# Prompt attention with undivided probabilities: the division moved from the probability rows to the weighed sums

## The chip, the cores and the metric

One core of a Trainium2 chip. The time is what the device takes for one execution of the program, in microseconds (us). A core has TensorE (matrix products, PE in the profile, its weight loads PEld), VectorE (DVE), ScalarE (ACT), GpSimd (POOL) and SyncE (SP, which issues all DMAs here). SBUF is the on-chip memory of 128 partitions; PSUM has 8 banks of 512 f32 for each partition and takes TensorE's results.

## The reference, cut to what matters

One layer of a decoder with two token mixers, for a prompt of 1024 tokens and 8 samples of 8 tokens each. The change touches the prompt's attention only:

```python
def block(args):
    i, qlb, qrb = args
    s = (jnp.einsum('bqhr,bkr->bhqk', qlb, c_kv)
         + jnp.einsum('bqhp,bkp->bhqk', qrb, k_r)).astype(jnp.float32)
    qpos = i * Q_BLOCK + jnp.arange(Q_BLOCK)
    s = jnp.where(kpos[None, :] <= qpos[:, None], s, -jnp.inf)
    p = jax.nn.softmax(s, axis=-1).astype(c_kv.dtype)
    return jnp.einsum('bhqk,bkr->bqhr', p, c_kv)
...
a = jnp.einsum('bshr,rhv->bshv', o_lat, w_uv).reshape(B, S, MLA_WIDTH)
```

There are 8 heads; everything is f32. A softmax divides exp(s - max) by its sum over the keys, one sum for each query and head.

## The kernel before, in words

The program works through stages: input norms and projections, prompt attention, the samples' attention, the output projection, the feed-forward part (gate and up, then down) and the last norm. A product of f32 matrices is made of three products of split operands (`mm3`, lines 873 to 875: high by high, low by high, high by low); the high part is a copy (`hi` on ScalarE, line 1425), the low part a subtraction on VectorE or POOL.

Prompt attention is cut into 16 units (`UNITS`). Unit u belongs to the pair of heads u // 4, to head u // 2 % 2 of that pair, and to the block of 512 queries u % 2 (block 0 or 1). A block has four query tiles of 128 (qi 0 to 3), and block 0 sees four key tiles (kt), block 1 eight. Because of the causal mask, query tile qt needs only its first qt + 1 key tiles, so row 3 of a unit is 512 columns wide in block 0 and 1024 in block 1.

For each query tile: `score` on TensorE makes the scores in one of two pairs of PSUM banks, VectorE takes their maximum (L2113) and scales it (L2116), ScalarE makes the exponential into the SBUF tile `prob` and sums it in its accumulator (L1578, an ACTIVATE and an ACTIVATION_READ_ACCUMULATOR), and VectorE inverts the sum (L2102). Then the row of probabilities is multiplied by the inverse: rows 0 to 2 on POOL (`normalise`, L782), row 3 on VectorE (L2107). For each key tile, `turn` transposes the probabilities on TensorE (L1096) into PSUM bank 4 or 5, ScalarE copies the high part to `pTH` and VectorE subtracts to get `pTL` (L2129); `product` multiplies them by the values `hvH`, `hvL`, two key tiles later in TensorE's order, and adds up in PSUM bank 6 or 7 (by the unit's parity). The result, 64 rows by 512 queries, goes to `aT` by a ScalarE copy (`move_weighed`) during key tile 1 of the next unit.

The order on each engine is written out by hand. While unit u is weighed, the scores, maxima and exponentials of unit u + 1 are made, one query tile for each key tile (`row_at`): at key tiles 0 to 3, and in the last unit of a pair (u % 4 == 3) at key tiles 4 to 7, as its first four key tiles carry the query and key projections of the next pair (`query_key`, `move_gen`, `query_hi`, and `query_lo` on POOL). After such a unit come the values of the next pair (`values`). Before the last unit, TensorE makes the samples' queries (L1131). Every engine runs its own list in order; semaphores join them. TensorE's `turn(0)` of a unit waits for the multiplied rows (`s_pn`, `s_pd`), a `turn` or `product` for the subtraction of the tile (`t_free`), `product(0)` for the accumulator's release (`o_free`). DMAs are all issued by SyncE; attention itself needs few.

Of the kernel before, what the change touches and what calls it, by code (L numbers as in the profile page):

```python
# [22 lines left out]
ALU = mybir.AluOpType  # L23
# [107 lines left out]
def build(nc, d):  # L131
    ctx = ExitStack()
    with ctx:
# [28 lines left out]
        mx, nmx, sm, rsm = (small.put(n, [P, 4]) for n in ("mx", "nmx", "sm", "rsm"))  # L162
# [93 lines left out]
        ukT = Region(R0).put("ukT", [NOPE, H, KVR])  # L256

# [53 lines left out]
        def sem(name):  # L311
# [34 lines left out]
        s_ready, s_mx, s_nm, s_exp, s_rc, s_pn, s_pd = (  # L346
            sem("s_" + n) for n in ("ready", "mx", "nm", "exp", "rc", "pn", "pd"))
# [313 lines left out]
        def _(pool):  # L661
# [114 lines left out]
            def normalise(u):  # L776
                for qi in range(3):
                    r, qt = 4 * u + qi, 4 * (u % 2) + qi
                    n = P * (qt + 1)
                    row = prob[:, prob_at(qt):prob_at(qt) + n]  # L780
                    pool.wait_ge(s_rc, r + 1)
                    pool.tensor_tensor(row, row, rsm[:, r % 4:r % 4 + 1].broadcast_to((P, n)),  # L782
                                       ALU.mult).then_inc(s_pn, 1)

# [10 lines left out]
            normalise(0)  # L795
            for u in range(UNITS):
                p = u // 4
                if u % 4 == 3 and u < UNITS - 1:
                    query_lo(p + 1)
                if u < UNITS - 1:  # L800
                    normalise(u + 1)
                if u == 0:
                    pool.wait_ge(out_ckv, 16)
                    pool.wait_ge(n2_lo, 2 * NC)
                    for z in qz:
                        pool.memset(z[:, :, :, :], 0.0).then_inc(made_z, 1)
                if u % 4 == 3 and p + 2 < PAIRS:
                    head_pieces(p + 2)
# [61 lines left out]
        def _(pe):  # L870
# [209 lines left out]
            def weigh(u):  # L1080
# [5 lines left out]
                def turn(kt):  # L1086
                    x = tr_count(u) + kt
                    if x >= 2:
                        pe.wait_ge(t_free, x - 1)
                    for qi in range(max(0, kt - 4 * blk), 4):  # L1090
                        if kt == 0 and qi < 3:
                            pe.wait_ge(s_pn, 3 * u + qi + 1)
                        elif kt == 0:
                            pe.wait_ge(s_pd, u + 1)
                        at = prob_at(4 * blk + qi) + P * kt
                        last = nc.tensor.transpose(ps[:, 4 + x % 2, P * qi:P * qi + P], prob[:, at:at + P],  # L1096
                                                   ident[:, :])
                    last.then_inc(t_ready, 1)

                def product(kt):  # L1100
                    x = tr_count(u) + kt
                    c0 = P * max(0, kt - 4 * blk)
                    pe.wait_ge(t_free, x + 1)
                    if kt == 0 and u >= 2:
                        pe.wait_ge(o_free, u - 1)
                    mm3(ps[:, 6 + u % 2, c0:512], hvH[:, kt, :], hvL[:, kt, :], pTH[:, x % 4, c0:512],
                        pTL[:, x % 4, c0:512], kt == 0, kt == nk - 1).then_inc(pv_x, 1)

                for kt in range(nk + 2):
# [9 lines left out]
                    if kt >= 2:  # L1119
                        product(kt - 2)  # L1120
                    if qi is not None and row_late(u, kt):
                        score(u + 1, qi)
# [300 lines left out]
        def _(act):  # L1423
# [159 lines left out]
            def move_weighed(u):  # L1583
                p, hh, blk = u // 4, u // 2 % 2, u % 2
                act.wait_ge(pv_x, tr_count(u + 1))
                part = slice(VH * hh, VH * hh + VH)
                hi(aT[part, p, 512 * blk:512 * blk + 512], ps[part, 6 + u % 2, :]).then_inc(o_free, 1)

            def move_turned(u):
                blk = u % 2  # L1590
                for kt in range(4 * (blk + 1)):
# [12 lines left out]
                    if kt == 1 and u:  # L1604
                        move_weighed(u - 1)
# [27 lines left out]
            move_weighed(UNITS - 1)  # L1633
# [253 lines left out]
        def _(dve):  # L1887
# [206 lines left out]
            def invert(r):  # L2094
                s = slice(r % 4, r % 4 + 1)
                dve.wait_ge(s_exp, r + 1)
                u, qi = r // 4, r % 4
                if u and qi < 3:
                    dve.wait_ge(s_pn, 3 * (u - 1) + qi + 1)
                elif u:  # L2100
                    dve.wait_ge(s_pd, u)
                nc.vector.reciprocal(rsm[:, s], sm[:, s]).then_inc(s_rc, 1)  # L2102
                if qi == 3:
                    qt = 4 * (u % 2) + 3
                    row = prob[:, prob_at(qt):prob_at(qt + 1)]
                    dve.wait_ge(s_rc, r + 1)
                    nc.vector.tensor_scalar(row, row, rsm[:, s], None, ALU.mult).then_inc(s_pd, 1)  # L2107
# [10 lines left out]
            def move_turned(u):  # L2118
                blk = u % 2
                for kt in range(4 * (blk + 1)):  # L2120
# [5 lines left out]
                    if qi:  # L2126
# [3 lines left out]
                                            pTH[:, x % 4, c0:512], ALU.subtract).then_inc(t_free, 1)  # L2130
                    for i in gens_at(u, kt):
                        move_gen(u // 4 + 1, i)
# [13 lines left out]
            for u in range(UNITS):  # L2146
                p = u // 4
                move_turned(u)
                if u % 4 == 3 and u < UNITS - 1:
                    move_values(p + 1)  # L2150

# [35 lines left out]
            dve.wait_ge(s_pn, 3 * UNITS)  # L2187
            dve.wait_ge(s_pd, UNITS)
# [466 lines left out]
```

## Time and profile before

| | us |
|---|---|
| median of three runs | 1470.52 (1469.29, 1470.52, 1474.88) |
| the profiled execution | 1473.64 |
| its span | 1471.7 |
| prompt attention in it, about | 292 to 526 |

The span runs from the first to the last recorded instruction. Busy shares are of this span; matmul and weight load overlap, so their shares are not added. The granted clock (PEclk) is 1.00 at 2.4 GHz and 0.50 at 1.2 GHz. "Idle before" is the time an engine waited just ahead of an instruction, with the engine and line that ended the wait. The stage around the change is 16% of the span; behind it lie 947 us of samples' attention, projections and feed-forward that the change does not touch.

### The profile page before, as it was taken

What the parts mean: (1) busy time and instruction counts of PE and PEld (TensorE: products, weight loads), DVE (VectorE), ACT (ScalarE), POOL (GpSimd) and SP (SyncE); (2) the same over time, 40 slices, a digit from 0 to 9 for tenths busy, and PEclk for the clock granted to TensorE, in tenths of its full rate; (3) what the DMA queues carried; (4) which work ended last, traced back from release to release, by engine and by line L of the source; (5) the groups of instructions that cost most, each with busy time, mean ns of one, the idle gap of its engine ahead of it and who ended that gap; (6) DMA issues with size and microseconds to landing.
All of it is one profiled execution on the core that took longest, in us unless ns stands there. A gap on an engine that the chain in (4) does not pass through costs nothing.

```text
span 1471.7 us, 23463 instructions
## 1 busy us (share of the span) xinstructions
PE 1354.1 (92%) x9216; PEld 1259.0 (86%) x9216; DVE 827.0 (56%) x1304; ACT 506.6 (34%) x870; POOL 439.4 (30%) x278
## 2 busy tenths in 40 slices
PE   6979998799999898999669999999999989999987
PEld 4758898688888765899659999999999989999987
DVE  4793114666666432514765454434445547989975
ACT  3412212455655431301332222222222224444452
POOL 1161222434333202154644444444444410000000
PEclk9989999899999899999779999999999999999998
DMA  7011010200003532442012222222222249766503
GB/s 230 3 46 59 25 34 4 70 1 19 1 15 117 188 115 112 163 141 94 4 37 74 74 88 80 73 80 76 69 73 73 88 159 368 266 194 229 196 1 122
DMA packets 64376, 142.10 MB, mean 97 GB/s; under 512 B 7490, under 2 KB 14530, under 8 KB 63586
## 3 DMA queue, kind: packets, MB, share of 16 engines
q1 hardware_dynamic: 64290, 140.93, 28.1%
q8 instruction: 57, 0.93, 0.3%
q14 instruction: 29, 0.24, 0.1%
HBM read 118.35 MB, written 22.55 MB: 96 GB/s over the span
## 4 chain that ended last, share of the span: by engine, by line
PE 71%; DVE 15%; issue 4%; DMA 4%; POOL 2%; ACT 2%; SPq 0%; DVEq 0%; POOLq 0%; ACTq 0%
PE ps L873 21%; PE ps L874 21%; PE ps L875 21%; DMA araw<-in_w_dn 2%; PE ps L1096 2%; PE ps L881 2%; DVE x L1890 2%; PE ps L1159 1%; DVE aHL L2442 1%; DMA x<-in_x 1%; DVE bHL L2445 1%; PE ps L1202 1%; DVE mx L2113 1%; DVE bsum L2434 1%; DVE mL L2227 1%
## 5 line engine op out<-in xcount | busy, mean ns | idle before, releaser
L827 POOL TENSOR_TENSOR ws<-wraw,ws 128x1024 fp32r<-128x1024 f32 x55 | 136.5, 2483 | 199.9 <-ACT ws L1425 199.9
L873 PE MATMUL ps<-bHL,aHL 128*128 128x272 f32 x616 | 180.2, 293 | 11.5 <-DVE bHL L2445 11.5
L875 PE MATMUL ps<-bHL,aHL 128*128 128x272 f32 x616 | 179.0, 291 | 0.0
L874 PE MATMUL ps<-bHL,aHL 128*128 128x272 f32 x616 | 178.8, 290 | 0.0
L873 PEld LDWEIGHTS ps<-bHL,aHL 128*128 128x128 f32 x616 | 117.8, 191 | 13.0 <-DVE bHL L2445 13.0
L2308 DVE TENSOR_TENSOR bufP<-bufP,ps 128x544 f32<-128x544 f32 x66 | 47.5, 721 | 139.3 <-PE ps L875 137.1
L1425 ACT ACTIVATE ws<-wraw 128x1024 fp32r<-128x1024 f32 x55 | 58.3, 1061 | 181.9 <-PE ps L875 181.9
L874 PEld LDWEIGHTS ps<-bHL,aHL 128*128 128x128 f32 x616 | 117.8, 191 | 0.0
L875 PEld LDWEIGHTS ps<-bHL,aHL 128*128 128x128 f32 x616 | 117.6, 191 | 0.0
L827 POOL TENSOR_TENSOR ws<-wsum,ws 128x1024 fp32r<-128x1024 f32 x22 | 64.8, 2946 | 66.2 <-ACT ws L1425 66.2
L865 POOL TENSOR_TENSOR rt<-ms,mhalf 128x3 f32<-128x3 f32 (+1 forms) x3 | 3.1, 1039 | 265.3 <-DVE ms L2474 265.3
L2129 DVE TENSOR_TENSOR pTL<-ps,pTH 128x512 fp32r<-128x512 f32 (+1 forms) x96 | 53.1, 554 | 46.3 <-ACT pTH L1425 44.8
L782 POOL TENSOR_TENSOR prob<-prob,rsm 128x128 f32<-128x128 f32 (+5 forms) x48 | 49.7, 1042 | 96.7 <-DVE rsm L2102 96.7
L2308 DVE TENSOR_TENSOR bufC<-bufP,ps 128x544 f32<-128x544 f32 x42 | 30.3, 720 | 80.3 <-PE ps L875 72.9
L1425 ACT ACTIVATE aHL<-araw 128x512 fp32r<-128x512 f32 x66 | 41.7, 631 | 89.1 <-DVE araw L2417 59.9
L1425 ACT ACTIVATE pTH<-ps 128x512 fp32r<-128x512 f32 (+1 forms) x96 | 46.9, 490 | 52.1 <-PE ps L1096 51.1
L1096 PE MATMUL ps<-ident,prob 128*128 128x128 f32 x288 | 54.2, 295 | 11.5 <-DVE prob L2107 7.4
L873 PE MATMUL ps<-x4H,ws 128*128 128x272 f32 x176 | 52.3, 297 | 7.4 <-POOL x4L L832 7.4
L873 PE MATMUL ps<-x3H,ws 128*128 128x272 f32 x176 | 51.8, 294 | 6.9 <-DVE x3L L2278 6.9
L1578 ACT ACTIVATE prob<-ps,nmx 128x128 f32<-128x128 f32 (+3 forms) x64 | 47.4, 741 | 28.9 <-DVE nmx L2116 28.9
L873 PE MATMUL ps<-x1H,ws 128*128 128x272 f32 x176 | 52.2, 297 | 5.2 <-POOL x1L L832 5.2
L2113 DVE TENSOR_REDUCE mx<-ps 128x1 f32<-128x128 f32 (+3 forms) x64 | 48.1, 751 | 12.5 <-PE ps L1077 12.2
(356 smaller groups left out, 4509.9 us busy)
## 6 DMA issues: line engine op xcount, KB each, us to landing
araw<-in_w_dn SPq DMA_DIRECT2D x121, 256.0 KB, 3.3
wraw<-in_w_gu SPq DMA_DIRECT2D x44, 512.0 KB, 3.6
cp<-in_cache SPq DMA_DIRECT2D x64, 272.0 KB, 4.7
ab<-acts SPq DMA_DIRECT2D x34, 272.0 KB, 4.9
acts<-bufC SPq DMA_DIRECT2D x22, 272.0 KB, 2.1
x<-in_x SPq DMA_DIRECT2D x4, 1088.0 KB, 8.1
x2s<-x SPq DMA_DIRECT2D x8, 544.0 KB, 9.2
x<-x2s SPq DMA_DIRECT2D x8, 544.0 KB, 6.2
```

The costliest lines, as they stand in the source:

```text
L782: pool.tensor_tensor(row, row, rsm[:, r % 4:r % 4 + 1].broadcast_to((P, n)), ALU.mult).then_inc(s_pn, 1)
L827: pool.tensor_tensor(w[:, 1, :], w_source(j), w[:, 0, :], ALU.subtract).then_inc(cw_lo, 1)
L873: nc.tensor.matmul(out, wh, xh, start=start, stop=False)
L874: nc.tensor.matmul(out, wh, xl, start=False, stop=False)
L875: return nc.tensor.matmul(out, wl, xh, start=False, stop=stop)
L881: last = nc.tensor.matmul(ps[:, bank, 0:n], ones[:, :], sq[:, kk, 0:n], start=kk == 0, stop=kk == k - 1)
L1096: last = nc.tensor.transpose(ps[:, 4 + x % 2, P * qi:P * qi + P], prob[:, at:at + P], ident[:, :])
L1425: return nc.scalar.activation(out, x, ACT.Copy, scale=scale)
L1578: nc.scalar.activation(prob[:, prob_at(qt):prob_at(qt) + n], psf[:, 1024 * (r % 2):1024 * (r % 2) + n], ACT.Exp, bias=nmx[:, s:s + 1], sca ...
L2113: nc.vector.tensor_reduce(mx[:, s], psf[:, at:at + P * (qt + 1)], AX.X, ALU.max).then_inc(s_mx, 1)
L2129: nc.vector.tensor_tensor(pTL[:, x % 4, c0:512], ps[:, 4 + x % 2, c0:512], pTH[:, x % 4, c0:512], ALU.subtract).then_inc(t_free, 1)
L2308: nc.vector.tensor_tensor(halves(out[:, g, :]), halves(x[:, g, :]), pair(b + 2 * g), ALU.add).then_inc(added, 1)
```

## The change

Probabilities stay undivided. POOL's `normalise` and VectorE's multiplication of row 3 go. `turn(0)` waits for the exponentials. The inverse sums get eight columns, so that two units can hold theirs. At key tile 3 of a unit, behind `turn(3)` and `product(1)`, TensorE makes four transpositions (`row_factors`): the stationary operand is one column of inverse sums repeated 128 times, the moving one the identity, so that each of the 128 output rows holds the inverse sums of the 128 queries. They go to the PSUM bank that held the accumulator of the unit before. ScalarE copies 64 of these rows to `rinv` (`move_factors`, key tile 3), and no longer moves the weighed sums. VectorE does this now, multiplying them by `rinv` as it reads them (`move_weighed`, behind its subtraction at key tile 1 of the next unit).

```diff
-        mx, nmx, sm, rsm = (small.put(n, [P, 4]) for n in ("mx", "nmx", "sm", "rsm"))
+        mx, nmx, sm = (small.put(n, [P, 4]) for n in ("mx", "nmx", "sm"))
+        rsm = small.put("rsm", [P, 8])
...
+        rinv = Region(R0 + 1024).put("rinv", [P, 512])
...
-            def normalise(u):
-                for qi in range(3):
-                    r, qt = 4 * u + qi, 4 * (u % 2) + qi
-                    n = P * (qt + 1)
-                    row = prob[:, prob_at(qt):prob_at(qt) + n]
-                    pool.wait_ge(s_rc, r + 1)
-                    pool.tensor_tensor(row, row, rsm[:, r % 4:r % 4 + 1].broadcast_to((P, n)),
-                                       ALU.mult).then_inc(s_pn, 1)
...
-                        if kt == 0 and qi < 3:
-                            pe.wait_ge(s_pn, 3 * u + qi + 1)
-                        elif kt == 0:
-                            pe.wait_ge(s_pd, u + 1)
+                        if kt == 0:
+                            pe.wait_ge(s_exp, 4 * u + qi + 1)
...
-                    if kt == 0 and u >= 2:
-                        pe.wait_ge(o_free, u - 1)
+                    if kt == 0 and u:
+                        pe.wait_ge(s_rk, u)
...
+                def row_factors():
+
+                    pe.wait_ge(s_rc, 4 * u + 4)
+                    if u:
+                        pe.wait_ge(o_free, u)
+                    for qi in range(4):
+                        i = 4 * (u % 2) + qi
+                        last = nc.tensor.transpose(ps[:, 7 - u % 2, P * qi:P * qi + P],
+                                                   rsm[:, i:i + 1].broadcast_to((P, P)), ident[:, :])
+                    last.then_inc(s_rt, 1)
...
                     if kt >= 2:
                         product(kt - 2)
+                    if kt == 3:
+                        row_factors()
...
-            def move_weighed(u):
-                p, hh, blk = u // 4, u // 2 % 2, u % 2
-                act.wait_ge(pv_x, tr_count(u + 1))
-                part = slice(VH * hh, VH * hh + VH)
-                hi(aT[part, p, 512 * blk:512 * blk + 512], ps[part, 6 + u % 2, :]).then_inc(o_free, 1)
+            def move_factors(u):
+                act.wait_ge(s_rt, u + 1)
+                hi(rinv[VH:P, :], ps[VH:P, 7 - u % 2, :]).then_inc(s_rk, 1)
...
-                    if kt == 1 and u:
-                        move_weighed(u - 1)
+                    if kt == 3:
+                        move_factors(u)
...
             def invert(r):
-                s = slice(r % 4, r % 4 + 1)
                 dve.wait_ge(s_exp, r + 1)
-                u, qi = r // 4, r % 4
-                if u and qi < 3:
-                    dve.wait_ge(s_pn, 3 * (u - 1) + qi + 1)
-                elif u:
-                    dve.wait_ge(s_pd, u)
-                nc.vector.reciprocal(rsm[:, s], sm[:, s]).then_inc(s_rc, 1)
-                if qi == 3:
-                    qt = 4 * (u % 2) + 3
-                    row = prob[:, prob_at(qt):prob_at(qt + 1)]
-                    dve.wait_ge(s_rc, r + 1)
-                    nc.vector.tensor_scalar(row, row, rsm[:, s], None, ALU.mult).then_inc(s_pd, 1)
+                if r >= 8:
+                    dve.wait_ge(s_rt, r // 4 - 1)
+                nc.vector.reciprocal(rsm[:, r % 8:r % 8 + 1], sm[:, r % 4:r % 4 + 1]).then_inc(s_rc, 1)
+
+            def move_weighed(u):
+                p, hh, blk = u // 4, u // 2 % 2, u % 2
+                dve.wait_ge(pv_x, tr_count(u + 1))
+                dve.wait_ge(s_rk, u + 1)
+                part = slice(VH * hh, VH * hh + VH)
+                nc.vector.tensor_tensor(aT[part, p, 512 * blk:512 * blk + 512], ps[part, 6 + u % 2, :], rinv[VH:P, :],
+                                        ALU.mult).then_inc(o_free, 1)
...
+                    if kt == 1 and u:
+                        move_weighed(u - 1)
```

## Rows read from the trace of the kernel before

**Rows 1.** The page, part 1: busy time, share of the span, instructions.
```profile
PE 1354.1 (92%) x9216; PEld 1259.0 (86%) x9216; DVE 827.0 (56%) x1304; ACT 506.6 (34%) x870; POOL 439.4 (30%) x278
```
**Rows 2.** Stretches, all engines: length, busy us (instructions), PEclk, DMA share, GB/s.
```profile
292.00:526.00 234.00, 216.30 (x1305) 188.99 (x1306) 145.43 (x329) 131.75 (x301) 75.66 (x74) 0.94 0.16 54
```
**Rows 3.** Waits of TensorE in 292:526: us in total, times, longest.
```profile
PE ps L1096 <- DVE prob L2107: 7.4, 5, 2.0
```
**Rows 4.** Timeline of TensorE, gaps: start, length, instruction [idle before].
```profile
303.66 0.33 PE L1096 MATMUL ps<-ident,prob 128*128 128x128 f32 x1 [2.00 <-DVE prob L2107]
...
363.52 0.47 PE L1096 MATMUL ps<-ident,prob 128*128 128x128 f32 x1 [1.74 <-DVE prob L2107]
...
503.96 4.92 PE L1131 MATMUL ps<-qs,ukT 64*128 64x64 f32 x32 [2.10 <-ACT prob L1578]
```
**Rows 5.** Timeline, VectorE and ScalarE ahead of the gap's end in unit 5.
```profile
359.84 1.22 DVE L2113 TENSOR_REDUCE mx<-ps 128x1 f32<-128x1024 f32 x1
...
361.27 1.11 ACT L1578 ACTIVATE prob<-ps,nmx 128x1024 f32<-128x1024 f32 x1 [1.68 <-DVE nmx L2116]
...
362.29 0.19 ACT L1578 ACTIVATION_READ_ACCUMULATOR prob<-ps,nmx 128x1 f32 x1
...
362.71 0.75 DVE L2107 TENSOR_SCALAR prob<-prob,rsm 128x1024 f32<-128x1024 f32 x1
```
**Rows 6.** Timeline, the same steps before units 1, 0 and 15.
```profile
302.17 0.19 ACT L1578 ACTIVATION_READ_ACCUMULATOR prob<-ps,nmx 128x1 f32 x1
302.60 1.01 DVE L2107 TENSOR_SCALAR prob<-prob,rsm 128x1024 f32<-128x1024 f32 x1
...
292.29 0.19 ACT L1578 ACTIVATION_READ_ACCUMULATOR prob<-ps,nmx 128x1 f32 x1
293.25 0.33 PE L1096 MATMUL ps<-ident,prob 128*128 128x128 f32 x1 [0.22 <-DVE prob L2107]
...
503.62 0.19 ACT L1578 ACTIVATION_READ_ACCUMULATOR prob<-ps,nmx 128x1 f32 x1
```
**Rows 7.** VectorE's groups by shape in 292:526: busy us, mean ns, idle before.
```profile
L2081 DVE TENSOR_TENSOR kL<-ps,kH 64x512 fp32r<-64x512 f32 x12 | 8.2, 685 | 0.2
```
**Rows 8.** Timeline of VectorE in unit 4, key tiles 1 and 2.
```profile
356.14 0.54 DVE L2129 TENSOR_TENSOR pTL<-ps,pTH 128x384 fp32r<-128x384 f32 x1
356.84 1.09 DVE L2113 TENSOR_REDUCE mx<-ps 128x1 f32<-128x896 f32 x1 [0.15 <-PE ps L1077]
```
**Rows 9.** Timeline of TensorE: four transpositions and the product behind them.
```profile
310.29 0.60 PE L1096 MATMUL ps<-ident,prob 128*128 128x128 f32 x4
310.65 0.48 PE L873 MATMUL ps<-pTH,hvH 128*128 128x512 f32 x1
```
**Rows 10.** Line 1096 alone: ns min/median/max, first and last start.
```profile
L1096 PE MATMUL ps<-ident,prob x288: 270/273/475, 292.2 to 523.9; 128*128 128x128 f32 x144
```
**Rows 11.** ScalarE's groups by shape in 292:526.
```profile
L1425 ACT ACTIVATE aT<-ps 64x512 f32<-64x512 f32 x16 | 9.4, 586 | 1.1 <-PE ps L875 1.0
```
**Rows 12.** Timeline, unit 3: ScalarE at key tile 4, TensorE's wait behind.
```profile
340.12 0.58 ACT L1425 ACTIVATE pTH<-ps 128x512 fp32r<-128x512 f32 x1
...
342.45 0.41 PE L873 MATMUL ps<-kH,qH 128*128 128x384 f32 x1 [0.59 <-ACT prob L1578]
```
**Rows 13.** Timeline, unit 5: ScalarE's copy of tile 4, TensorE's product 4.
```profile
370.12 0.59 ACT L1425 ACTIVATE pTH<-ps 128x512 fp32r<-128x512 f32 x1
...
371.79 0.48 PE L873 MATMUL ps<-pTH,hvH 128*128 128x512 f32 x1
```
**Rows 14.** Stretches behind two gaps, as in rows 2: the clock.
```profile
362.50:366.50 4.00, 2.98 (x14) 2.98 (x15) 2.75 (x9) 1.79 (x5) 0.40 (x1) 0.57 0.02 4
57.00:61.50 4.50, 2.95 (x17) 2.24 (x16) 2.44 (x6) 0.40 (x1) 0.85 (x1) 1.00 0.00 0
```
**Rows 15.** Timeline of TensorE: two other gaps.
```profile
287.85 0.66 PE L873 MATMUL ps<-kH,qH 128*128 128x384 f32 x1 [1.64 <-ACT prob L1578]
...
59.55 0.71 PE L889 MATMUL ps<-diag,ones 128*128 128x128 f32 x4 [1.55 <-DVE diag L1919]
```

More of the change, by code:

```diff
@@ L343, in build @@
         vg_ready, vg_hi, vg_free = sem("vg_ready"), sem("vg_hi"), sem("vg_free")
-        s_ready, s_mx, s_nm, s_exp, s_rc, s_pn, s_pd = (
-            sem("s_" + n) for n in ("ready", "mx", "nm", "exp", "rc", "pn", "pd"))
+        s_ready, s_mx, s_nm, s_exp, s_rc, s_rt, s_rk = (
+            sem("s_" + n) for n in ("ready", "mx", "nm", "exp", "rc", "rt", "rk"))
         t_ready, t_hi, t_free, pv_x, o_free = (sem(n) for n in ("t_ready", "t_hi", "t_free", "pv_x", "o_free"))
@@ L794, in _ @@
             head_pieces(1)
-            normalise(0)
             for u in range(UNITS):
@@ L799, in _ @@
                     query_lo(p + 1)
-                if u < UNITS - 1:
-                    normalise(u + 1)
                 if u == 0:
@@ L1632, in _ @@
                     move_values(p + 1)
-            move_weighed(UNITS - 1)
             def sample_exp(g):
@@ L2150, in _ @@
                     move_values(p + 1)
+            move_weighed(UNITS - 1)
             def sample_max(g):
@@ L2185, in move_latents @@
                         "p (b h t) -> p b h t", b=2, h=H)).then_inc(o4, 1)
-            dve.wait_ge(s_pn, 3 * UNITS)
-            dve.wait_ge(s_pd, UNITS)
+            dve.wait_ge(s_rt, UNITS)
             def scale_heads(c, bank):
```

## The prediction

> **What bounds the kernel now.** I read the page first: TensorE is busy 92% of the span [rows 1]. Then the stretches: prompt attention fills 292 to 526 us, TensorE busy 216.3 of 234 us at a mean granted clock of 0.94, VectorE 145 us, ScalarE 132 us [rows 2]. So TensorE bounds this stretch, with gaps, and every instruction added to it is paid unless it falls in a gap. The waits say what ends the gaps: the largest single one is 7.4 us on the VectorE multiplication of row 3 (L2107) [rows 3]. The timeline puts them in place. Units go in fours of about 60 us. Unit 1 of a four (units 1, 5, 9, 13) opens with a gap: TensorE restarts at 303.66 and 363.52 after gaps of 2.00 and 1.74 us, each with a shorter wait on POOL just before it. Unit 15 opens with a 2.10 us gap that an exponential ends, not a multiplication [rows 4]. Only these four gaps can shrink; units 3, 7 and 11 open with score and query products of the next pair as cover, and the units of block 0 follow long products.
>
> **The four gaps.** In unit 5 the chain is: maximum over 1024 (359.84, 1.22 us), exponential (361.27, 1.11 us), its accumulator read (ends 362.48), reciprocal, multiplication (362.71, 0.75 us), transposition at 363.52 [rows 5]. After the change the transposition waits for the accumulator read alone. Before unit 15 that step takes from 503.81 to 503.96, 0.15 us [rows 4, 6], so here it could start at 362.63: 0.9 us earlier. In unit 1 the read ends at 302.36, the transposition started at 303.66 and could start at 302.5: 1.15 us earlier (the multiplication took 1.01 us there). In unit 0 the read ends 292.48 and the fourth transposition came at 293.25: 0.6 us earlier [rows 6]. POOL's 48 multiplications end no gap that would outlast this.
>
> But the maximum itself comes later in units 4, 8 and 12. VectorE now moves the weighed sums of the unit before, right behind its subtraction of key tile 1, and ahead of the maximum over 896. The nearest row for that move is a TENSOR_TENSOR of 64x512 from PSUM with an SBUF operand, 0.685 us [rows 7]. Between the subtraction's end (356.68) and the maximum (356.84, after 0.15 us of waiting on TensorE) VectorE has 0.3 us at most, counting overlaps [rows 8]; so some 0.4 us runs down the chain through the two maxima and two exponentials behind it. Gain there 0.9 - 0.4 = 0.5 us, three times. Unit 0 has no move, unit 1 keeps its 1.15. Together: -0.6 - 1.15 - 1.5 = -3.25 us. What is late next in all of them is the exponential.
>
> **Added on TensorE.** 64 transpositions, four a unit. Four of the same shape at the full clock take from 310.29 to the product at 310.65: 0.36 us [rows 9]; I take 0.4. Their stationary operand is one column repeated, which no row shows; the bounds are nothing (all in gaps) and 0.475 us each, the longest of the 288 [rows 10], 30 us in all; I take the near row because shape and moving operand are the same. In units 0, 4, 8, 12 and 14 they stand before a gap that VectorE and ScalarE end, so they are hidden. In 3, 7 and 11 they are hidden too, but by a wait that the next part makes longer. Paid in eight units: +3.2 us. If the cover of the five goes, +2.0 more. Their own waits cost nothing: the reciprocals are done before the unit opens, and the accumulator is freed two key tiles earlier. Behind them in TensorE's queue stand turn 4 and product 2.
>
> **Moved on ScalarE.** A copy of 64x512 leaves key tile 1 and another enters at key tile 3, both 0.586 us [rows 11]: no change in busy time, but in place. In units 3, 7 and 11 ScalarE is the late one exactly there: it starts the copy of turned tile 4 at 340.12, back to back with the query work, and TensorE then waits 0.59 us for exponential 0 of the next unit, until 342.45 [rows 12]. The new copy goes in between: 3 x 0.6 = +1.8 us. In units 1, 5, 9 and 13 it stands between exponential 3 and the copy of tile 4. That copy started at 370.12 [rows 13]; now maximum 3 is 0.3 to 0.5 us later (the move on VectorE) and the copy goes behind both, near 371.0; its subtraction (0.69) ends near 372.3, while turn 6, which needs it, would be ready some 0.4 us sooner (TensorE reaches product 4 at 371.79 now, 0.26 us behind turn 6, and 0.4 later with the added four). At the opening of these units the copy of the unit before also stands ahead of the first turned tile, some 0.3 us. I take 0.7 us, four times: +2.7 us rounded; bounds 0 (the VectorE multiplication of row 3 is gone at the same place and may pay for all of it) and 1.2 us each.
>
> **Unit 14.** The VectorE move delays the chain of maxima by some 0.6 us and the gap before unit 15 gets nothing back, since it waits for the exponential already: +0.6 us. POOL: its queue only gets shorter, and its query work stands in the same order. DMA queues are not touched.
>
> **The clock.** Behind each of the four gaps the granted clock is at 1.2 GHz for a while: 0.57 in the mean over 362.5 to 366.5, so some 3.4 of these 4 us [rows 14]. A gap of 1.64 us at 287.85 was followed by such a fall, one of 1.55 us at 59.55 was not, the clock staying 1.00 [rows 14, 15]. The gap before unit 1 shrinks to about 0.9 us, those before 5, 9 and 13 to about 1.4. Work of 3.4 us at half clock costs TensorE 1.7 us, but here ScalarE and VectorE stand close behind, and I let half of that come back to them: 0.9 us for each fall that stays out. I take unit 1 and one more: -1.8 us.
>
> Sum: -3.25 + 3.2 + 1.8 + 2.7 + 0.6 - 1.8 = +3.2 us. The profiled execution took 1473.64 us (span 1471.7 and 1.9 around it), so 1476.8; it is 3.1 us above the median of the three runs, 1470.52, and measured against that the forecast is 1473.7 us.
>
> A rule on the multiplication that goes: the Trainium skill, "SBUF — State Buffer", section "Who interferes with whom", says that VectorE and GpSimd share one port pair as an exclusive lock, taken by fp32 tensor_scalar in its two-port mode. The trace agrees as far as it goes: the same 1024 columns took 0.75 us in unit 5 and 1.01 in unit 1 [rows 5, 6]. By that rule the POOL work that goes frees nothing else, for the VectorE instructions that stay read PSUM; without it one could hope for a VectorE that is faster throughout.
>
> **Rivals.**
> 1. The clock falls behind all four gaps as before. For it: the gap of 1.4 us is close to the 1.64 that was followed by a fall, and new short gaps stand behind it. Against: unit 1, with 0.9. Sum +5.0: 1475.5 us. Chance 0.25.
> 2. Faster side: no fall is left and ScalarE and VectorE keep their places at no cost: -3.25 + 3.2 - 4 x 1.7 = -6.9: 1463.6 us. For it: a multiplication that goes took VectorE 0.75 us at 1024 columns, as much as a move brings. Against: it goes from the gap, and the move comes where VectorE is full. Chance 0.08, of which 0.03 beyond 0.5%.
> 3. Slower side: VectorE becomes the bound in block 0. There it worked without a break over two key tiles [rows 8]. If each of the 15 moves with work behind it is paid at 0.685, that is 10.3 us; with the transpositions (3.2), ScalarE (1.8) and the gains of units 0 and 1 (-1.75): +13.6, 1484.1 us. It decides from six full moves more than I count. Against it: even there VectorE waited 0.15 us for TensorE, and the multiplication that goes stood at the head of the same queue. Chance 0.12.
> 4. The transpositions of a repeated column are dear: 0.475 us each in 11 units, 20.9 us in place of 3.2: 1491 us. Nothing in the profile speaks for it. Chance 0.03.
> That the stalls don't move at all, since something other than the multiplication ends them, is excluded by the 0.06 us between its end and the transposition [rows 5].
>
> **The numbers.** The forecast has 0.52; its own range is 1471 to 1477. The range that takes in rivals 1, most of 2 and the near part of 3 is 1467 to 1482. About 0.5% (7.4 us) is what a measurement of this kernel can tell from no change. Faster by more: 0.03. Slower by more: 0.09 from rival 3 and 0.03 from rival 4. The rest, 0.85, is within it.
>
> **What would show it.** Right: the longest gap before units 5, 9 and 13 at 1.3 to 1.5 us, ended by the exponential; before unit 1 about 0.9; the four added transpositions some 0.4 us from the first to what follows; the wait near 342.45 grown to about 0.8; a new wait of 0.3 to 0.5 us at turn 6 of units 1, 5, 9, 13, ended by the subtraction. Wrong: VectorE moves of over 1 us, added transpositions that take longer than the others, a mean clock over attention above 0.97 (rival 2), or VectorE named at waits all over block 0 (rival 3).

## The result, and the profile after

The changed kernel takes 1477.00 us in the median of 20 runs, the kernel before 1472.74 in the median of 20: a ratio of 1.0027, 95% interval 1.0017 to 1.0037. By the ratio that is 4.0 us more, where 3.2 more were forecast; the interval leaves out 1, and the difference is below the half per cent that the prediction named as what a measurement can tell from no change.

The page after, parts 1 (busy time, share of the span, instructions) and 2 (the granted clock in 40 slices):

```profile
PE 1357.4 (92%) x9280; PEld 1263.1 (86%) x9280; DVE 822.8 (56%) x1304; ACT 508.6 (35%) x870; POOL 389.8 (26%) x230
...
PEclk8999999899999899999779999999999999999988
```

Against [rows 1]: POOL has 48 instructions and 50 us less, TensorE 64 instructions more. VectorE and ScalarE have kept their number of instructions and nearly their busy time. What changed is the place of the work.

The stretches of attention, and the four that lie behind the openings of units 1, 5, 9 and 13 (columns as in [rows 2]):

```profile
292.00:526.00 234.00, 214.49 (x1347) 188.02 (x1345) 138.59 (x325) 131.59 (x298) 25.54 (x26) 0.96 0.16 54
304.50:308.50 4.00, 4.00 (x27) 3.22 (x25) 2.69 (x9) 3.16 (x8) 0.00 (x0) 1.00 0.00 0
362.00:366.00 4.00, 3.52 (x23) 3.20 (x23) 3.66 (x10) 2.63 (x9) 0.00 (x0) 1.00 0.00 0
422.00:426.00 4.00, 3.53 (x25) 3.06 (x24) 3.20 (x11) 2.62 (x9) 0.00 (x0) 1.00 0.00 0
482.00:486.00 4.00, 3.52 (x23) 3.06 (x23) 3.20 (x9) 2.95 (x8) 0.00 (x0) 1.00 0.62 235
```

None of the four falls to 1.2 GHz is left in this execution, where [rows 14] had 0.57 over 4 us. The kernel is slower all the same. The waits of TensorE in 292:500 say where (us in total, times, longest):

```profile
PE ps L863 <- ACT prob L1579: 7.0, 12, 1.3
PE ps L1084 <- ACT prob L1579: 4.5, 4, 1.2
PE ps L1084 <- DVE pTL L2126: 2.8, 4, 0.9
```

The same stretch before had the 7.4 us of [rows 3] and two more that compare:

```profile
PE ps L873 <- ACT prob L1578: 3.1, 9, 0.6
PE ps L1096 <- POOL prob L782: 0.9, 4, 0.2
```

The waits on the multiplications are gone (8.3 us); 4.5 us on the exponentials stand at the same four places. But the scores (L863) wait 3.9 us more for an exponential to leave their bank, and a new wait of 2.8 us for VectorE's subtractions has come. The two in detail, timeline of all engines after (start, length, instruction [idle before]): first unit 3 at key tiles 3 and 4, then unit 1 at key tile 6:

```profile
337.32 0.60 ACT L1426 ACTIVATE rinv<-ps 64x512 f32<-64x512 f32 x1
337.94 0.60 ACT L1426 ACTIVATE pTH<-ps 128x512 fp32r<-128x512 f32 x1
...
340.29 0.41 PE L863 MATMUL ps<-kH,qH 128*128 128x384 f32 x1 [1.32 <-ACT prob L1579]
```
```profile
308.51 1.16 DVE L2126 TENSOR_TENSOR pTL<-ps,pTH 128x512 fp32r<-128x512 f32 x2 [1.08 <-ACT pTH L1426]
309.25 0.44 PE L1084 MATMUL ps<-ident,prob 128*128 128x128 f32 x2 [0.65 <-DVE pTL L2126]
```

In unit 3 the copy of the inverse sums (`rinv`) stands ahead of the copy that in [rows 12] began at once, and the wait of 0.59 us has become 1.32. In unit 1 TensorE waits 0.65 us at turn 6, where it waited for nothing before.

The opening of unit 5, which answers to [rows 5]:

```profile
358.11 1.21 DVE L2110 TENSOR_REDUCE mx<-ps 128x1 f32<-128x1024 f32 x1
...
359.55 1.11 ACT L1579 ACTIVATE prob<-ps,nmx 128x1024 f32<-128x1024 f32 x1 [1.68 <-DVE nmx L2113]
360.56 0.19 ACT L1579 ACTIVATION_READ_ACCUMULATOR prob<-ps,nmx 128x1 f32 x1
360.77 0.60 ACT L1426 ACTIVATE rinv<-ps 64x512 f32<-64x512 f32 x1
...
360.80 0.33 PE L1084 MATMUL ps<-ident,prob 128*128 128x128 f32 x1 [1.21 <-ACT prob L1579]
```

The transposition follows the end of the accumulator read (360.75) by 0.05 us, and the copy of the inverse sums stands on ScalarE just where the first turned tile will want it.

**Units, measured.** From here on the length of unit u is the time from the start of the last product of unit u - 1 to the start of its own last product (for unit 0 from the first score product). These are differences of starts in TensorE's timeline. "0 to 14" is their sum, "15" the last unit, of which more than half is spent at 1.2 GHz in every kernel. Each row is one profiled execution; columns of three units give their mean.

| kernel, profile | 1 | 5 | 9 | 13 | 2, 6, 10 | 3, 7, 11 | 4, 8, 12 | 0 to 14 | 15 |
|---|---|---|---|---|---|---|---|---|---|
| before | 14.50 | 13.55 | 14.33 | 13.70 | 8.53 | 22.86 | 14.23 | 216.2 | 23.5 |
| before, again | 14.59 | 13.72 | 14.34 | 13.81 | 8.52 | 22.86 | 14.23 | 216.4 | 23.5 |
| after | 12.82 | 13.58 | 13.26 | 13.27 | 8.94 | 23.49 | 14.66 | 217.8 | 25.4 |
| after, again | 12.82 | 13.56 | 14.22 | 14.21 | 8.94 | 23.47 | 14.65 | 219.5 | 23.8 |
| no division | 11.83 | 11.82 | 11.82 | 11.83 | 8.51 | 22.77 | 14.22 | 206.4 | 25.1 |
| + factors | 11.74 | 11.74 | 11.74 | 11.74 | 8.95 | 22.72 | 14.65 | 209.4 | 23.5 |
| + VectorE move | 12.27 | 12.32 | 12.31 | 12.30 | 8.67 | 22.83 | 14.61 | 210.4 | 25.2 |
| before, gaps filled | 13.19 | 12.97 | 12.91 | 12.93 | 8.50 | 22.85 | 14.23 | 212.0 | 26.6 |
| copy moved | 11.84 | 12.61 | 12.28 | 12.28 | 8.93 | 23.18 | 14.65 | 212.8 | 23.7 |
| VectorE move at end | 13.09 | 13.09 | 14.67 | 14.53 | 8.94 | 23.48 | 14.66 | 220.1 | 23.6 |
| both moved | 11.48 | 11.45 | 11.29 | 11.29 | 8.52 | 23.22 | 14.64 | 207.7 | 25.6 |
| copy last | 11.48 | 11.46 | 11.31 | 11.30 | 8.51 | 22.78 | 14.65 | 206.5 | 25.6 |

From the first score to the samples' first score, attention took 240.2 and 240.3 us before, 243.7 and 243.8 after: 3.5 us more in both pairs, and the fifteen units and the last share it differently. Behind attention both kernels take 946 to 947 us.

What differs in the last unit is the clock. Unit 15 in the kernel before, after, and after again (columns as in [rows 2]):

```profile
501.35:524.85 23.50, 19.15 (x102) 14.03 (x101) 6.75 (x12) 9.53 (x18) 1.38 (x1) 0.71 0.54 190
501.52:526.93 25.41, 21.23 (x106) 15.87 (x105) 6.45 (x12) 10.13 (x19) 0.00 (x0) 0.66 0.49 175
505.14:528.93 23.79, 19.59 (x106) 14.17 (x105) 6.46 (x12) 10.12 (x19) 0.00 (x0) 0.71 0.53 187
```

From these mean clocks, about 13.6, 17.3 and 13.8 us of the unit are at 1.2 GHz. In both profiles of the kernel with filled gaps (26.63 us, mean clock 0.62) it is about 20.2. So the table's last column must be read apart from the others: it moves by up to 3 us with the clock alone.

### The profile page after: what moved, and what is told of

The parts are those of the page before. It is cut to its first block, busy times and chain, and to the rows that moved or that the text cites. A ratio compares the mean times of both kernels' runs of the same rounds, so it can differ in the third digit from the quotient of the medians.

```text
span 1473.6 us, 23571 instructions
## 1 busy us (share of the span) xinstructions
PE 1357.4 (92%) x9280; PEld 1263.1 (86%) x9280; DVE 822.8 (56%) x1304; ACT 508.6 (35%) x870; POOL 389.8 (26%) x230
## 4 chain that ended last, share of the span: by engine, by line
PE 68%; DVE 17%; issue 5%; DMA 4%; ACT 3%; POOL 2%; SPq 0%; DVEq 0%; POOLq 0%; ACTq 0%
PE ps L863 20%; PE ps L864 20%; PE ps L865 20%; DMA araw<-in_w_dn 2%; PE ps L871 2%; DVE mx L2110 2%; DVE x L1888 2%; DVE pTL L2126 1%; DMA x<-in_x 1%; PE ps L1084 1%; PE ps L1160 1%; DVE aHL L2441 1%; DVE bHL L2444 1%; PE ps L1203 1%; DVE mL L2226 1%
## 5 line engine op out<-in xcount | busy, mean ns | idle before, releaser
L863 PE MATMUL ps<-bHL,aHL 128*128 128x272 f32 x616 | 181.5, 295 | 8.2 <-DVE bHL L2444 8.1
L863 PEld LDWEIGHTS ps<-bHL,aHL 128*128 128x128 f32 x616 | 119.0, 193 | 9.8 <-DVE bHL L2444 9.8
L864 PEld LDWEIGHTS ps<-bHL,aHL 128*128 128x128 f32 x616 | 119.0, 193 | 0.0
L865 PEld LDWEIGHTS ps<-bHL,aHL 128*128 128x128 f32 x616 | 118.8, 193 | 0.0
L679 POOL TENSOR_TENSOR rt<-ms,mhalf 128x3 f32<-128x3 f32 x16 | 13.7, 856 | 176.5 <-DVE ms L1908 176.5
L1084 PE MATMUL ps<-ident,prob 128*128 128x128 f32 x288 | 50.8, 285 | 10.3 <-DVE pTL L2126 5.1
L863 PE MATMUL ps<-x4H,ws 128*128 128x272 f32 x176 | 52.3, 297 | 7.5 <-POOL x4L L822 7.5
L775 POOL TENSOR_TENSOR qL<-qt,qH 128x384 fp32r<-128x384 f32 (+1 forms) x24 | 21.9, 921 | 139.0 <-ACT qH L1426 138.8
L863 PE MATMUL ps<-x3H,ws 128*128 128x272 f32 x176 | 51.8, 294 | 6.8 <-DVE x3L L2277 6.8
L863 PE MATMUL ps<-x1H,ws 128*128 128x272 f32 x176 | 52.1, 296 | 5.2 <-POOL x1L L822 5.2
```

The costliest lines, as they stand in the source:

```text
L863: nc.tensor.matmul(out, wh, xh, start=start, stop=False)
L864: nc.tensor.matmul(out, wh, xl, start=False, stop=False)
L865: return nc.tensor.matmul(out, wl, xh, start=False, stop=stop)
```

## The experiments

All ratios are to the kernel before, run on the same chip.

**No division.** What the change could bring if nothing were put in for it.

```diff
-                    if kt == 3:
-                        row_factors()
...
-            def move_factors(u):
+            def move_weighed(u):
```
(This `move_weighed` is ScalarE's plain copy at key tile 1, as before. VectorE's goes; the probabilities stay undivided.)

> The changed kernel with the division left out altogether (the output is not the reference's): no transpositions of the inverse sums, no copy of them, the weighed sums moved undivided by ScalarE at key tile 1 as before. Length of attention = first score product to the samples' first score product; 240.2 us before, 243.6 after. Theory P (each thing put in is paid at its place on TensorE's queue, the shortened gaps win back less): about 8 us less than after, near 233 to 236, since 64 transpositions (16 x 0.4), the ScalarE copy at key tile 3 and the VectorE move all go; unit 5 (last product of unit 4 to last product of unit 5) near 12.5 us against 13.6. Rival V (VectorE's move alone is the payer): the same kernel, no difference from P here, but p2 would be as fast as this one. Rival N (what goes is worth nothing, the gain in the gaps is given back at once): 239 to 240. Time against before: P 0.995 to 0.997, N 1.000.

1465.21 us, ratio 0.9946 (0.9929 to 0.9963); attention 232.0 us against 243.7, so 11.7 less where about 8 were expected (unit 5 at 11.82, where 12.5 was). What the change takes away is worth 9.8 us in units 0 to 14 (216.2 to 206.4); rival N falls. What it puts in costs 11.4 (206.4 to 217.8).

**Transpositions only.** The kernel above with `row_factors` at key tile 3, unread.

> As p1, with the 64 transpositions on TensorE put back (key tile 3, same waits), their result unread; weighed sums undivided by ScalarE. Against p1: P: units 2, 6, 10 and 14 longer by 0.4 us each, units 4, 8, 12 too, units 3, 7, 11 by 0 to 0.4, units 1, 5, 9, 13 by 0 to 0.4 net; attention +4 to +5 us. V: +0 to +1. Rival R (a repeated column is dear to load): 0.8 us or more for each four, +10 us.

1464.90 us, ratio 0.9944 (0.9919 to 0.9970). Units 0 to 14: +3.0 us, less than the +4 to +5 expected. Units of block 0 are 0.44 us longer each; the gap behind 4, 8 and 12 takes that back and leaves units 1, 5, 9 and 13 0.09 us shorter, their own four included; 3, 7, 11 hide theirs. A repeated column loads as any other (0.133 to 0.138 us a load in the changed kernel), so rival R falls. The time of the program did not follow the 3.0 us: it is that of the kernel without division, and in its profile unit 15 is 1.6 us shorter (23.5 against 25.1).

**VectorE's move only.**

```diff
-                dve.wait_ge(s_rk, u + 1)
-                nc.vector.tensor_tensor(aT[...], ps[part, 6 + u % 2, :], rinv[VH:P, :],
+                nc.vector.tensor_tensor(aT[...], ps[part, 6 + u % 2, :], kr[VH:P, 0:512],
```

> As p1, with VectorE moving the weighed sums (a multiplication by another resident tile, 64x512, same place), no transpositions and no ScalarE copy; the output is not the reference's. Against p1: P: the gaps before units 5, 9, 13 and 15 grow by 0.4 to 0.6 us each as the maxima come later, the rest hides: +1.5 to +2.5 us. V: +6 to +10 us, VectorE named at waits in block 0.

1469.62 us, ratio 0.9972 (0.9957 to 0.9987). Units 0 to 14: +4.0 us, about twice theory P and half of V. Units 1, 5, 9 and 13 take 0.5 us more each and units 4, 8 and 12 0.4 more. P was also wrong on where: the gap before units 5, 9 and 13 is 1.21 us and that before unit 15 is 2.10 us with the move and without it.

**The gaps filled.** The kernel before, with work for TensorE in the four gaps.

```diff
                     for qi in range(max(0, kt - 4 * blk), 4):
+                        if kt == 0 and qi == 3 and u % 4 == 1:
+                            if u >= 2:
+                                pe.wait_ge(o_free, u - 1)
+                            for _ in range(6):
+                                nc.tensor.matmul(ps[:, 6 + u % 2, :], hvH[:, 0, :], hvH[:, 0:4, :],
+                                                 start=True, stop=True)
```

> The kernel before, with six products of 128x512 (their result is overwritten) put into the gap before the fourth transposition of units 1, 5, 9 and 13, nothing else changed. Theory C (the fall of the clock behind the gaps is what costs, 1.7 us each): the granted clock stays at 1.00 behind all four and units 1, 5, 9, 13 shrink by 1.5 to 1.7 us each, 6 to 7 us in all. P, by the unit lengths of after (unit 1 -1.7, unit 9 -1.1, unit 13 -0.4, unit 5 0.0): ScalarE and VectorE take half of it back, 0.5 to 1.0 us each, 2 to 4 us in all, with new waits on them in the first four key tiles. If the filler runs past the gap's end by 0.2 us it takes that back.

Its stretches and TensorE's timeline at the opening of unit 1:

```profile
306.00:310.00 4.00, 3.75 (x26) 3.28 (x25) 3.39 (x10) 3.30 (x10) 1.02 (x2) 1.00 0.01 2
364.00:368.00 4.00, 3.75 (x25) 3.28 (x26) 3.01 (x11) 3.35 (x9) 0.81 (x2) 1.00 0.00 0
```
```profile
303.12 1.64 PE L1095 MATMUL ps<-hvH 128*128 128x512 f32 x6
305.37 0.33 PE L1102 MATMUL ps<-ident,prob 128*128 128x128 f32 x1 [0.61 <-DVE prob L2113]
```

The gap is as long as it was, but only 0.61 us of it idle, and the clock stays at 2.4 GHz in all four places. Units 1, 5, 9, 13 shrink by 1.3, 0.6, 1.4 and 0.8 us: 4.1 us, 1.0 each in the mean, at the top of what P allows; units 1 and 9 come near C's lower end of 1.5, units 5 and 13 do not. The time does not follow: 1473.18 us, ratio 0.9999 (0.9982 to 1.0016), where the interval would still allow 2.7 us of gain. Unit 15 took 3.1 us longer, so that attention as a whole shrank by 1.1 us, less than the interval can show.

**The ScalarE copy in other places.** The changed kernel with:

```diff
-                    if kt == 3:
+                    if kt == (2 if u % 4 == 3 else 3):
                         row_factors()
...
+                        if u % 2 == 0 and kt == 3:
+                            move_factors(u)
                         exponential(u + 1, qi)
-                    if kt == 3:
+                    if kt == (2 if u % 4 == 3 else 7):
                         move_factors(u)
```

> The changed kernel with only the place of the ScalarE copy of the inverse sums changed: in block 0 ahead of exponential 3 instead of behind it, in units 1, 5, 9, 13 behind the last turned tile, in units 3, 7, 11, 15 at key tile 2 (their transpositions at key tile 2 too). Reference points, sum of units 0 to 14: before 216.2, after 217.8, without division 206.4, with transpositions 209.4, with the VectorE move alone 210.4 us. Theory S (the copy's place in ScalarE's order is the largest part of what is put in): units 3, 7, 11 return from 23.49 to 22.85, units 1, 5, 9, 13 fall from 12.8 to 13.6 to 12.2 to 12.4, waits on the subtraction at turn 6 are gone; sum 211.5 to 213. Rival V (VectorE's move holds the same places back): units 1, 5, 9, 13 stay above 12.8; sum 215 or more. Time, S: 0.3 to 0.4% below after.

1468.67 us, ratio 0.9969 (0.9958 to 0.9979). TensorE's waits in 292:500:

```profile
PE ps L1084 <- ACT prob L1579: 4.5, 4, 1.2
PE ps L863 <- ACT prob L1579: 3.8, 12, 0.6
```

The 2.8 us on the subtractions are gone and those at the scores are back from 7.0 to 3.8. Units 0 to 14: 212.8, 5.0 us less than after. Theory S holds, with misses: 3, 7 and 11 return only to 23.18, unit 5 to 12.61, unit 1 goes further than expected, to 11.84, and the time is 0.6% below after where 0.3 to 0.4 were expected. The profile of after has 1.7 us more in unit 15 than this one, so it flatters the difference in attention as a whole. In units 3, 7, 11 and 15 the transpositions moved along with the copy; that is a second change (see the last experiment but one).

**VectorE's move in another place.**

```diff
-                    if kt == 1 and u:
-                        move_weighed(u - 1)
...
+                    if u % 2 == 0 and kt == 3:
+                        move_weighed(u)
...
                 move_turned(u)
+                if u % 2:
+                    move_weighed(u)
```

> The changed kernel with only the place of VectorE's move of the weighed sums changed: at the end of its own unit, where VectorE waits for the exponential (block 0) or for the next score (block 1), instead of key tile 1 of the next. Theory V: the 4.0 us that the move cost when it was added alone come back: units 4, 8, 12 from 14.65 to 14.65 or less, units 1, 5, 9, 13 shorter by 0.4 to 0.5 each, unit 15 earlier by 0.5; sum of units 0 to 14 near 214.5 to 215.5. Theory S: under 1 us comes back, since the ScalarE copy holds the same waits: 217 or more.

1477.54 us, ratio 1.0018 (1.0002 to 1.0034): the same as after. Units 0 to 14 take 220.1 us; the clock falls in units 9 and 13 here, so the profile to compare with is after, again, 219.5. Theory V falls: with the copy where it is, moving VectorE's work wins nothing. The gap is shorter (0.85 us), and what it wins is lost again at the next score, where after waited 0.47 us:

```profile
363.16 0.33 PE L1084 MATMUL ps<-ident,prob 128*128 128x128 f32 x1 [0.85 <-ACT prob L1579]
365.72 0.41 PE L863 MATMUL ps<-kH,qH 128*128 128x384 f32 x1 [1.35 <-ACT prob L1579]
```

**Both moved**, with the transpositions behind turn 1 in units 1, 2, 5, 6, 9, 10, 13, 14.

```diff
-                    if kt == 3:
+                    if kt == (2 if u % 4 == 3 else 1 if u % 4 in (1, 2) else 3):
                         row_factors()
```

> Both changes of place together, and the four transpositions put where TensorE waits anyway (behind turn 1 in units 1, 2, 5, 6, 9, 10, 13, 14). If ScalarE's and VectorE's places are all that was lost, the sum of units 0 to 14 is that of the kernel with transpositions and nothing else (209.4 us) or up to 1.5 us less, and the time that of p1 and p2, 0.994 to 0.996 of before. If one of them only hides the other's cost elsewhere: 212 or more, 0.998.

1468.29 us, ratio 0.9966 (0.9951 to 0.9981), a little above the 0.994 to 0.996 expected; units 0 to 14 at 207.7, at the low end of what was expected. Against the kernel with the ScalarE copy moved, units 5, 9 and 13 are 1.0 to 1.2 us shorter: with the copy out of the way, VectorE's move and the transpositions do bring something in these units. How much each of the two brings was not taken apart, and the time of the program does not show it (0.9969 and 0.9966): unit 15 is 1.9 us longer in this profile.

**The kernel before once more.**

> The kernel before, unchanged, profiled once more. The filler that kept the clock up in the first four gaps (p4) shortened attention by 1.1 us in its profile and units 1, 5, 9, 13 by 4.1, but left the median where it was. Theory C1 (the clock falls behind these four gaps in each execution): four falls again, units 1, 5, 9, 13 at 13.5 to 14.5 us. Theory C2 (whether it falls depends on the execution, and the first profile had more than the usual number): two falls or fewer, the units without a fall near 12.9, unit 15 longer or shorter by a multiple of 1.7 us.

One execution, 1471.87 us. All four falls again, the units within 0.2 us of the first profile: this fits C1, as far as two executions can tell.

**The copy last.** As with both moved, and in units 3, 7, 11 the transpositions back at key tile 3 and the copy behind exponential 3 (key tile 7).

```diff
-                    if kt == (2 if u % 4 == 3 else 1 if u % 4 in (1, 2) else 3):
+                    if kt == (1 if u % 4 in (1, 2) else 3):
                         row_factors()
...
-                    if kt == (2 if u % 4 == 3 else 7):
+                    if kt == (3 if u == UNITS - 1 else 7):
                         move_factors(u)
```

> As p7, but in units 3, 7 and 11 the transpositions are back at key tile 3 and the ScalarE copy stands at key tile 7, behind exponential 3 of the next unit (unit 15: both at key tile 3). Theory S: with the transpositions alone units 3, 7, 11 were 22.72 us, in p7 they are 23.20 to 23.25, so the copy at key tile 2 is what stands in the way: 22.7 to 22.8 now, sum of units 0 to 14 near 206.3 (p7 207.7), below the kernel that leaves the division out (206.4) by a hair. Rival: the transpositions at key tile 2 or VectorE's move hold these units: 23.1 or more again, sum 207.7. Time: 0.9955 to 0.9970 of before.

1465.15 us, ratio 0.9948 (0.9933 to 0.9963): faster than both kernels, by 8 and by 12 us, with the whole computation done. Units 3, 7, 11 at 22.78, as expected; units 0 to 14 at 206.5, as much as without division (206.4). That kernel is no strict bound, though: units 1, 5, 9 and 13 are 0.35 to 0.53 us shorter here than there, since its own ScalarE copy still stands at key tile 1 (this reason was not tested), and units 4, 8 and 12 are 0.43 longer. Against both moved, units 0 to 14 are 1.2 us shorter, and the intervals of the two times overlap.

The number came out, but the reason given for it, the copy at key tile 2, does not. The edit moved the transpositions back as well, so the run cannot tell the two apart; the profile of both moved can. Its unit 3, ScalarE's copy and the copy behind it, then TensorE at key tile 2:

```profile
331.33 0.59 ACT L1426 ACTIVATE rinv<-ps 64x512 f32<-64x512 f32 x1
333.34 0.60 ACT L1426 ACTIVATE pTH<-ps 128x512 fp32r<-128x512 f32 x1 [1.41 <-PE ps L1084]
...
329.36 0.60 PE L1104 MATMUL ps<-ident,rsm 128*128 128x128 f32 x4
329.71 0.42 PE L863 MATMUL ps<-cqH,w1H 128*128 128x384 f32 x1
```

Behind the copy of the inverse sums ScalarE idles for 1.41 us, so the copy at key tile 2 holds nothing. The transpositions do: TensorE works without a gap around them, and turn 3 starts 14.57 us behind the last product of unit 2, against 14.08 in the copy last. At key tile 3, behind the projections, they are covered: the wait of 0.19 us for VectorE's `qt` that both moved has before a score there is gone. The wait at the score behind it is nearly the same, 0.61 and 0.56 us. So the 0.44 us that units 3, 7 and 11 gained belongs to the transpositions' place, and the rival that the expectation named for them is the one that the profile bears out. The same holds for their 23.18 us when the ScalarE copy was moved (wait 0.59 us). TensorE's waits in 292:500 with the copy last:

```profile
PE ps L1084 <- ACT prob L1579: 3.4, 4, 0.8
PE ps L1132 <- ACT prob L1579: 2.1, 1, 2.1
PE ps L863 <- ACT prob L1579: 1.9, 4, 0.6
```

**The changed kernel and the filled one once more.**

> The changed kernel, unchanged, profiled once more. Its unit 15 took 25.41 us against 23.50 before, the other fifteen 1.6 us more than before. Theory U1 (what the clock does in unit 15 goes with the kernel's own timing): 25.4 again, attention 243.6. Theory U2 (it goes with the execution): 23.5 to 23.7 or 25.4 to 26.6 at random; the fifteen units the same within 0.3 us, no fall of the clock in them.

> The kernel before with the filled gaps, unchanged, profiled once more. U1: unit 15 at 26.6 again, so that it gives back 3.1 of the 4.2 us won in units 1, 5, 9 and 13, which would explain a median of 1473.2 against 1472.8. U2: 23.5 as often as 26.6, and the median stays unexplained by it.

One execution each, 1477.66 and 1477.19 us. After, again: two of the four falls are back, behind the openings of units 9 and 13 (0.64 and 0.57 over 4 us), and unit 15 took 23.8; attention 243.8 as before.

```profile
302.00:306.00 4.00, 3.26 (x22) 2.88 (x23) 2.95 (x9) 3.36 (x10) 0.00 (x0) 1.00 0.01 4
362.00:366.00 4.00, 2.95 (x20) 2.66 (x21) 2.65 (x9) 3.51 (x10) 0.00 (x0) 1.00 0.00 0
424.00:428.00 4.00, 3.53 (x15) 3.11 (x14) 3.44 (x10) 2.68 (x8) 0.00 (x0) 0.64 0.00 0
486.00:490.00 4.00, 3.81 (x13) 3.41 (x14) 3.56 (x10) 2.38 (x7) 0.00 (x0) 0.57 0.18 68
```

The filled kernel repeated itself to 0.02 us in each unit, unit 15 at 26.63 again. So for the filled kernel U1 holds, and unit 15 gives back three of the four microseconds, with some 6.6 us more at 1.2 GHz than before; for the changed one neither does as written: the parts vary, the sum did not. Why unit 15 should answer to time won ahead of it is not settled; two profiles of each kernel don't show it.

## Why the prediction was right, step by step

The time, its sign and its size were right (+3.2 forecast, +4.0 measured), and so was the mechanism in kind: gains in the gaps and of the clock, outweighed by what is put in. The terms were less so. Two errors went opposite ways, and unit 15, where the forecast had 1 us for other reasons, made up the rest by its clock. So the closeness of the number is in part luck.

- **The gaps, -3.25 us.** Right in kind and place: the exponential ends them now. They are 0.85 us before unit 1 (about 0.9 forecast) and 1.21 before 5, 9 and 13; the 1.3 to 1.5 named there does not fit the forecast's own terms, 1.74 - 0.5 = 1.24. Unit 0 won 0.63 us without the added work (0.6 forecast). In units 1, 5, 9 and 13 the shorter wait alone, from the filled kernel to the one without division, is 1.4, 1.2, 1.1 and 1.1 us, against 1.15 and 0.9.
- **VectorE's delay of 0.4 us in that term** was the size seen at the opening of unit 5: 0.85 us of gap with the move elsewhere, 1.21 with it. But the move costs 4.0 us alone in units 0 to 14, of which the forecast counted about 1.2 there; the 0.5 us in each of units 1, 5, 9 and 13 were partly in the term on the copy and the move below.
- **Unit 14, +0.6.** Too large. From the last product of unit 13 to the restart behind the gap before unit 15 TensorE takes 11.13 us before and 11.31 after (11.11 with the division left out, 11.32 with the move added to that): 0.2 us.
- **Transpositions, +3.2 us.** Measured 3.0 on their own. Four take 0.44 us where they are paid, where [rows 9] gave 0.36 and the forecast took 0.4; they are hidden in the places that it named.
- **The copy in units 3, 7, 11, +0.6 each.** Measured +0.63 (22.86 to 23.49), and it is gone in the copy last (22.78), where the transpositions stand at key tile 3 as in after and the copy does not. The place was right: a copy started back to back in [rows 12] has no room in front of it. The sign named for it was not: the wait grew from 0.59 to 1.32 us, not to 0.8.
- **The copy and the move in units 1, 5, 9, 13, +0.7 each.** The term that was mis-sized most on this side. With both, these units take 12.8 to 13.6 us against 11.8 with neither (without a fall of the clock in either): +1.0, +1.8, +1.4 and +1.4, 5.6 us for the four. The forecast had 2.7 here (four times 0.7 is 2.8) and 1.2 of the move's cost in the gap term, 3.9 together; with the upper bound of 1.2 each it would be 6.0. The transpositions add nothing to these units (11.74 with them, 11.83 without). The wait at turn 6 was forecast at 0.3 to 0.5 us and is 0.65 to 0.85; the next score waits as well, 0.47 us where 0.24 stands with the copy moved; that is the copy ahead of the first turned tile.
- **The clock, -1.8 us.** The price was right for this kernel: units 9 and 13 take 14.22 and 14.21 us with the fall and 13.26 and 13.27 without it, so 0.95 us, 0.9 forecast. Half of TensorE's 1.7 us does come back: in the two units with the fall the wait at turn 6 is gone (1.5 us in all in place of 2.8). It is no constant: the kernel with VectorE's move at the end lost 1.4 to 1.6 us a fall (13.09 against 14.67 and 14.53). The count was right in one profile and not in the other: all four falls stayed out in the first, two in the second, units 1 and 5. The gap before unit 9 is 1.21 us in both. What the forecast put at nothing is the clock in unit 15, with some 3.7 us more at 1.2 GHz in the first profile, where the unit is 1.9 us longer, and 0.2 in the second (0.3 longer).

Sorted by side: what goes was forecast at 6.3 us (3.25 + 1.2 for VectorE's delay + 1.8 for the clock) and is worth 9.8, of which 4.1 the clock (by the filled gaps); what is put in was forecast at 9.5 (3.2 + 1.8 + 2.7 + 0.6 + 1.2) and costs 11.4 in the first profile of after, unit 15 not counted. The two errors, 3.5 and 1.9 us, have opposite signs. They leave units 0 to 14 at +1.6 us, and unit 15 adds 1.9; in the second profile it is +3.1 (219.5 against 216.4) and 0.3. That both come to 3.5 has no shown reason.

Rival 1 is refuted by both profiles: the clock did not fall four times. Rival 2 is refuted in its second half: the falls did stay out in one execution, and ScalarE and VectorE took it. Rival 3, VectorE as the bound, named an engine whose move costs a third of what is put in when it stands alone (4.0 of 11.4 us), but TensorE waits for VectorE's subtraction (up to 500 us of the span) only at turn 6 of units 1, 5, 9 and 13, not all over block 0, and moving that work alone brought nothing. Rival 4 is refuted by the transpositions alone. That VectorE would not be faster throughout was right: the subtractions of 128x512 took 0.690 us on the average before and 0.687 after.

## What to carry to other kernels

Work that is moved between engines is priced by the instruction that stands behind it, not by its own length: sixteen copies of 0.6 us cost 5 us more at key tile 3 than behind the last turned tile or ahead of an exponential that is waited for anyway (units 0 to 14; in units 3, 7, 11 and 15 the transpositions moved along, which the profile of both moved shows to cost, not to help). Look in the timeline for instructions that start back to back (nothing fits in front of them) and for those with "idle before" (there a copy is free). And when two engines hold the same wait, moving the wrong one alone shows nothing: 1.0018 with VectorE's work moved, as after (1.0027), and 0.9969 with ScalarE's. In the units VectorE's move paid only once ScalarE's copy was out of the way (together with the transpositions' place). And two things moved in one edit cannot be told apart by its time: it took the profile to see that the last 0.44 us of units 3, 7 and 11 came from the transpositions.

## What the hardware showed that was not expected

- Six products of 128x512 in a gap of some 2 us kept TensorE at 2.4 GHz, and the units behind them ran 0.6 to 1.4 us faster each, yet the median of the whole program did not move (0.9999, interval 0.9982 to 1.0016). The last unit of the stage was at 1.2 GHz for some 20.2 us instead of 13.6, in both profiles, and took 3.1 us longer. A clock regained in one place is not a gain until the end of the stage shows it.
- A gap of 1.21 us, with one of 0.47 behind it, is followed by a fall of the clock in one execution and not in another, at the same place of the same program (unit 9: 13.26 and 14.22 us).
- A stationary operand of one column repeated 128 times loads in 0.133 to 0.138 us, no longer than the ordinary f32 tile of probabilities (0.141 in the mean).
